# The K, V and Q projection of a hybrid decoder step as seven half-size products per column block

## What is computed

```python
def shared_kv(x, pos, g_kv, w_kv, k_gain):
    kv = jnp.einsum('btd,de->bte', rms_norm(x, g_kv), w_kv)
    kv = kv.reshape(B, T, 2, N_GROUPS, HEADS_PER_GROUP, HEAD_DIM)
    k = rotary(rms_norm(kv[:, :, 0], k_gain), pos)
    return k, kv[:, :, 1]
def project_q(x, pos, g, w_q, q_gain):
    q = jnp.einsum('btd,de->bte', rms_norm(x, g), w_q)
    return rotary(rms_norm(q, q_gain), pos) * (HEAD_DIM ** -0.5)
```

## Time and profile before

| | before |
|---|---|
| median of 3 runs | 2135.53 us (2135.42 to 2136.53) |
| span of the profiled execution | 2134.4 us |
| PE busy | 2106.5 us, 99% |
| DVE, ACT, POOL busy | 1533.9, 967.6, 559.0 us |
| projection on PE, first matmul to last | 766.66 to 1206.26 us |

### The profile page before, as it was taken

How to read it: one execution, slowest core, us unless ns; L and a number is a source line. 1 busy time by engine, 2 the same in 40 slices (tenths; PEclk the granted TensorE clock), 3 DMA queues, 4 the chain that set the end, 5 groups by cost and what they waited for, 6 DMA issues and landing times.

```text
span 2134.4 us, 42632 instructions
## 1 busy us (share of the span) xinstructions
PE 2106.5 (99%) x15883; PEld 1958.0 (92%) x15883; DVE 1533.9 (72%) x2321; ACT 967.6 (45%) x1797; POOL 559.0 (26%) x780
## 2 busy tenths in 40 slices
PE   7999999999999999999999999999999999999998
PEld 7999999999999987777777776899999999999998
DVE  4888888888755767457465588878888888875544
ACT  4655545555544542123122255645554554553342
POOL 1002232223100135455455301640213323311000
PEclk8999999999999999999999999999999999999999
DMA  6236777888986532432532785221567788899664
GB/s 195 90 95 161 199 198 193 207 193 234 300 276 195 181 110 85 158 100 84 169 114 93 228 243 159 70 90 55 155 191 196 193 210 195 198 291 303 194 209 142
DMA packets 237758, 371.02 MB, mean 174 GB/s; under 512 B 23687, under 2 KB 120615, under 8 KB 235734
## 3 DMA queue, kind: packets, MB, share of 16 engines
q1 hardware_dynamic: 196806, 258.73, 36.9%
q0 software_dynamic: 34960, 104.33, 22.0%
q10 hardware_dynamic: 5864, 6.25, 0.9%
HBM read 297.75 MB, written 168.07 MB: 218 GB/s over the span
## 4 chain that ended last, share of the span: by engine, by line
PE 95%; DVE 2%; ACT 1%; issue 0%; DMA 0%; POOL 0%; ACTq 0%; SPq 0%; DVEq 0%; POOLq 0%
PE ps L1255 42%; PE ps L1358 20%; PE ps L2164 6%; PE ps L2166 6%; PE ps L2165 6%; PE ps L2364 2%; PE ps L2434 2%; PE ps L2466 1%; PE ps L2447 1%; PE ps L424 1%; PE ps L2397 1%; PE ps L866 1%; PE ps L490 1%; PE ps L2426 1%; PE ps L2158 1%; PE ps L2159 1%
## 5 line engine op out<-in xcount | busy, mean ns | idle before, releaser
L1255 PE MATMUL ps<-hT,w 128*128 128x258 f32 x2752 | 458.2, 283 | 0.0
L1255 PEld LDWEIGHTS ps<-hT,w 128*128 128x128 f32 x2752 | 384.8, 189 | 0.5 <-ACT acc L1189 0.4
L1255 PE MATMUL ps<-lT,w 128*128 128x258 f32 x1376 | 276.3, 282 | 0.0
L1255 PE MATMUL ps<-hB,w 128*128 128x258 f32 x1344 | 229.3, 282 | 0.0
L2164 PE MATMUL ps<-wq,xh 128*128 128x512 f32 x576 | 227.6, 395 | 0.7 <-DVE wq L1948 0.7
L2166 PE MATMUL ps<-wq,xl 128*128 128x512 f32 x576 | 227.4, 395 | 0.0
L2165 PE MATMUL ps<-wq,xh 128*128 128x512 f32 x576 | 226.9, 394 | 0.0
L1255 PEld LDWEIGHTS ps<-lT,w 128*128 128x128 f32 x1376 | 213.3, 189 | 0.0
L1358 PE MATMUL ps<-gdh,wda 128*128 128x258 f32 x1184 | 198.8, 283 | 0.0
L1358 PE MATMUL ps<-gdh,wdb 128*128 128x258 f32 x1152 | 193.5, 284 | 0.1
L1255 PEld LDWEIGHTS ps<-hB,w 128*128 128x128 f32 x1344 | 191.0, 189 | 0.0
(11 more groups left out here) (350 smaller groups left out, 4714.7 us busy)
## 6 DMA issues: line engine op xcount, KB each, us to landing
stage<-in_w_up SPq DMA_DIRECT2D x176, 256.0 KB, 3.7
wsum<-in_w_down POOLq DMA_DIRECT2D x132, 256.0 KB, 5.3
gs<-cb SPq DMA_DIRECT2D x44, 516.0 KB, 7.0
stage<-wsum SPq DMA_DIRECT2D x88, 256.0 KB, 2.9
tsum<-gs POOLq DMA_DIRECT2D x66, 258.0 KB, 7.7
tsum<-gneg POOLq DMA_DIRECT2D x66, 258.0 KB, 8.4
stage<-in_w_down SPq DMA_DIRECT2D x58, 256.0 KB, 3.2
stage<-in_w_kv SPq DMA_DIRECT2D x24, 512.0 KB, 4.3
```

Of the source, the lines that this page charges most:

```text
L1255: mm = pe.matmul(ps[:, bank + c, 0:HB], w, m[:, c * HB:(c + 1) * HB], start=(first and i == 0), stop=(i == len(parts) - 1), skip_group_che ...
```

## The change

The projection becomes nine steps, PSTEPS, over (group, k or q or v), with the groups in order 1, 2, 0. In a step the 1024 prompt rows x 1024 inputs, and the 1024 x 512 weight block, are cut in quadrants (x into A11 to A22 of 512 rows x 512 inputs, the weights into B11 to B22 of 512 inputs x 256 columns), and seven products of half size are formed from them and from their sums S1 to S4 and T1 to T4 (the Winograd form of Strassen's scheme). A product is 4 row tiles x 4 x 3 matmuls of 256 columns, into two PSUM banks. The samples are multiplied straight, by 32 matmuls of 256 columns per step, in four pieces of eight, with the pieces of w that are in the ring anyway.

The order of the products is B11, T1, T2, B21, T3, T4, B22, and no product of step n + 1 stands before B22 of step n. Partial results move between banks as they are needed: `act_e1` copies banks 0-1 to 2-3 behind B11, `act_u2` and `act_u3` copy banks 2-3 to SBUF behind T2 and T3, and `dve_c22p`, `dve_c12p` add those copies to banks 4-5. T4 accumulates into banks 2-3 and so waits for u3; T1 of the next step starts banks 4-5 afresh and so waits for c12p. Four units of 512 rows x 256 columns (c11, c22, c21, c12) and one of the samples (S) come out of a step and are normed, rotated and stored as before, but in pieces of 128 x 1024. c22 comes out in the step; S, c21 and c12 are worked on in the next.

The sums of x are made in place by POOL (`pool_x_sum`) while the last FFN products run; x is therefore spilled to DRAM first, and loaded again during attention. Three weight slots (ring0 to ring2) rotate. In the first step PE also multiplies two matmuls of 512 columns that nothing reads. In a v step, DVE takes the sample scores 0 to 5 in that step and 6 and 7 in the next. The first tiles that the attention needs are turned by PE within the last step (`pe_first_turn`). Several semaphores are merged, which changes nothing of the order. The core of the diff:

```diff
         MT = [P] * 8 + [NS]
+        CW = QW // 2
+        GORDER = (1, 2, 0)
+        PSTEPS = [(g, u) for g in GORDER for u in range(3)]
+        LASTP = len(PSTEPS) - 1
+        ORDER_IN = ("B11", "T1", "T2", "B21", "T3", "T4", "B22")
+        PARTNER = {"B11": "A11", "T1": "S1", "T2": "S2", "B21": "A12", "T3": "S3", "B22": "S4", "T4": "A22"}
+        BANK = {"B11": 0, "B21": 0, "T1": 4, "B22": 4, "T2": 2, "T3": 2, "T4": 2}
+        UNITS = ("c11", "c22", "S", "c21", "c12")
+        BIG = ("c11", "c22", "c21", "c12")
...
+        def unit_made(n, name):
+            return {"c11": (pj_cp, 5 * n + 3), "c21": (pj_cp, 5 * n + 5), "c22": (pj_cs, 2 * n + 1),
+                    "c12": (pj_cs, 2 * n + 2), "S": (pj_k, 4 * n + 4)}[name]
...
+        def act_e1(act, n):
+            if n:
+                act.wait_ge(pj_cp, 5 * n)
+            else:
+                act.wait_ge(pj_ss, 1)
+            act_wide(act, ps[:, 2:4, :], ps[:, 0:2, :], (pj_pe, nth(n, "B11")))
+
+        def act_u2(act, n):
+            act.wait_ge(*((pj_cs, 2 * n) if n else (pj_ss, 2)))
+            act_wide(act, two(acc[:, 0:T]), ps[:, 2:4, :], (pj_pe, nth(n, "T2")))
+
+        def act_u3(act, n):
+            wait(act, pj_cs, 2 * n - 1)
+            act_wide(act, two(rb[:, 0:T]), ps[:, 2:4, :], (pj_pe, nth(n, "T3")))
...
+            for n in range(LASTP + 1):
+                last, normed = n == LASTP, PSTEPS[n][1] != 2
+                before = n and PSTEPS[n - 1][1] != 2
...
+                act_c11(act, n)
+                act_sample_low(act, n, 0)
+                if not last:
+                    act_scale(act, n + 1, "B12")
+                act_hi(act, n, "B22")
+                if normed and n:
+                    act_squares(act, n, "c11")
+                    act_root(act, n, "c11")
+                act_u3(act, n)
...
+                if not last:
+                    act_hi(act, n + 1, "B11")
+                    act_scale(act, n + 1, "B22")
+                if normed:
+                    act_squares(act, n, "c22")
+                    act_root(act, n, "c22")
...
+        def dve_c22p(v, n):
+            v.wait_ge(pj_cp, 5 * n + 4)
+            row_free(v, n, "c22")
+            nc.vector.tensor_tensor(two(row(n, "c22")), ps[:, 4:6, :], two(rb[:, 0:T]), ALU.add).then_inc(pj_cs, 1)
+
+        def dve_c12p(v, n):
+            v.wait_ge(pj_pe, nth(n, "B22"))
+            v.wait_ge(pj_cp, 5 * n + 2)
+            row_free(v, n, "c12")
+            nc.vector.tensor_tensor(two(row(n, "c12")), ps[:, 4:6, :], two(acc[:, 0:T]), ALU.add).then_inc(pj_cs, 1)
...
+            for n in range(LASTP + 1):
+                last, normed = n == LASTP, PSTEPS[n][1] != 2
+                before = n and PSTEPS[n - 1][1] != 2
+                gi = n // 3
+                if n:
+                    dve_weights_sum(v, n, "T2")
+                    dve_c12p(v, n - 1)
+                    dve_lo(v, n, "T2")
+                    if before:
+                        for name in ("S", "c21"):
+                            dve_mean(v, n - 1, name)
+                            dve_normed(v, n - 1, name)
+                        dve_lo(v, n, "B21")
+                        dve_weights_sum(v, n, "T3")
+                        dve_mean(v, n - 1, "c12")
+                        dve_normed(v, n - 1, "c12")
+                    else:
+                        for name in ("S", "c21"):
+                            dve_values(v, n - 1, name)
+                        dve_lo(v, n, "B21")
+                        dve_weights_sum(v, n, "T3")
+                        dve_values(v, n - 1, "c12")
+                        sample_scores(v, gi - 1, 6)
+                    dve_lo(v, n, "T3")
+                    dve_weights_sum(v, n, "T4")
+                    if not before:
+                        sample_scores(v, gi - 1, 7)
+                    dve_lo(v, n, "T4")
+                if not normed:
+                    dve_sample_add(v, n, 0)
+                    dve_values(v, n, "c11")
+                elif n:
+                    dve_lo(v, n, "B22")
+                    dve_mean(v, n, "c11")
+                    dve_sample_add(v, n, 0)
+                    dve_normed(v, n, "c11")
                 else:
...
+                    dve_sample_add(v, n, 0)
+                if not normed or n == 0:
+                    dve_lo(v, n, "B22")
+                dve_c22p(v, n)
+                if n == 0:
+                    dve_x_los("S4")
+                    dve_mean(v, n, "c11")
+                    dve_normed(v, n, "c11")
+                if not last:
+                    dve_lo(v, n + 1, "B11")
+                    dve_weights_sum(v, n + 1, "T1")
+                if normed:
+                    dve_mean(v, n, "c22")
+                    dve_normed(v, n, "c22")
+                else:
+                    dve_values(v, n, "c22")
+                    sample_scores(v, gi, 0)
+                    sample_scores(v, gi, 1)
+                if last:
+                    dve_masks(v)
+                    v.wait_ge(at_tp, 1)
+                    nc.vector.tensor_copy(qT[:, 0, :], ps[:, 6, :]).then_inc(at_tc, 1)
+                if not normed:
+                    sample_scores(v, gi, 2)
+                    sample_scores(v, gi, 3)
+                dve_sample_add(v, n, 1)
+                if last:
+                    v.wait_ge(at_tp, 2)
+                    nc.vector.tensor_copy(kT[:, 0, :], ps[:, 6, :]).then_inc(at_tc, 1)
+                else:
+                    dve_lo(v, n + 1, "T1")
+                if not normed:
+                    sample_scores(v, gi, 4)
+                    sample_scores(v, gi, 5)
+            dve_c12p(v, LASTP)
...
-                            pe.matmul(out, xh[:, k, tok], W, start=(k == 0), stop=False)
-                            pe.matmul(out, xh[:, k, tok], Wt, start=False, stop=False)
-                            mm = pe.matmul(out, xl[:, k, tok], W, start=False, stop=(k == KC - 1))
-                        mm.then_inc(pj_pe, 1)
...
+            def product(n, b):
+                pe.wait_ge(pj_l, nth(n, b))
+                if n == 0 or (n == 1 and b == "B11"):
+                    x_ready(b)
+                hi, lo = xq[PARTNER[b]]
+                w = wslot(n, b)
+                for t in range(KH):
+                    out = ps[:, BANK[b] + t // 2, t % 2 * CW:(t % 2 + 1) * CW]
+                    tok = slice(t * P, (t + 1) * P)
+                    for k in range(KH):
+                        cols = slice(k * CW, (k + 1) * CW)
+                        pe.matmul(out, hi[:, k, tok], w[:, 0, cols], start=(b in ("B11", "T1") and k == 0 and t % 2 == 0), stop=False,
+                                  skip_group_check=True)
+                        pe.matmul(out, hi[:, k, tok], w[:, 1, cols], start=False, stop=False, skip_group_check=True)
+                        mm = pe.matmul(out, lo[:, k, tok], w[:, 0, cols], start=False, stop=(k == KH - 1),
+                                       skip_group_check=True)
+                mm.then_inc(pj_pe, 1)
...
+            pe.wait_ge(f_xa, 6 * KH + 1)
+            for n in range(LASTP + 1):
+                if n:
+                    samples(n, "B11")
+                    pe.wait_ge(pj_cp, 5 * n - 2)
+                product(n, "B11")
+                if n == 0:
+                    pe.wait_ge(f_xa, 7 * KH)
+                    for c in range(2):
+                        pe.matmul(ps[:, 2 + c, :], xq["A11"][0][:, 0, 0:P], pre0[:, 0, 0:QW], start=True, stop=True)
+                    samples(0, "B11").then_inc(pj_ss, 1)
+                wait(pe, pj_cs, 2 * n)
+                product(n, "T1")
+                if n == 0:
+                    pe.wait_ge(split_acc, split[1].acc + 2 * KC - 2)
+                    for i in range(9):
+                        nm = pe.matmul(ps[0:MT[i], 7, i:i + 1], acc[:, i * P:i * P + MT[i]], ones[:, 0:1],
+                                       start=True, stop=True)
+                    nm.then_inc(pj_ss, 1)
+                pe.wait_ge(pj_cp, 5 * n + 1)
+                product(n, "T2")
+                samples(n, "B21")
+                product(n, "B21")
+                pe.wait_ge(pj_cp, 5 * n + 2)
+                product(n, "T3")
+                samples(n, "T3")
+                if n == LASTP:
+                    pe_first_turn(pe, 0)
+                pe.wait_ge(pj_cp, 5 * n + 4)
+                product(n, "T4")
+                samples(n, "B22")
+                if n == LASTP:
+                    pe_first_turn(pe, 1)
+                pe.wait_ge(pj_cs, 2 * n + 1)
+                product(n, "B22")
```

936 lines of the change are left out of this document (572 added, 364 removed).

## The result

| | before | after |
|---|---|---|
| median | 2135.48 us (4 runs, 2134.94 to 2136.53) | 2148.94 us (4 runs, 2146.43 to 2149.40) |
| ratio | 1 | 1.0063, 95% interval 1.0049 to 1.0078 |
| span of the profiled execution | 2134.4 us | 2144.6 us |

The account below looks back on a forecast made before the run. PE was taken as the bound, busy 2106.5 of 2134.4 us. Matmuls 400.2 + gates 10.2 + c12p 15.6 + step 8's end 8.0 + clock 5.1 = 439.1 against 439.6, so 2135.0 us; own forecast 2126 to 2144, range 2108 to 2160.

Parts of the forecast that it names:

- The matmuls: PE's projection: 3312 matmuls of 256 columns at 0.1197 us, 396.4 us, plus 3.8 of fixed parts, 400.2 without waits.
- the clock: PE at a lower clock after standing still: 1.7 us behind each long wait (after steps 2, 5, 8), 5.1 in all.
- My section on what costs nothing: Sums of x, spills and step 0's scaling fit under the last FFN products at no cost; up to 3 us if late.
- the waits for c12p behind v steps: T1 after steps 2 and 5 waits for c12p behind DVE's score rounds of 3.82 us: 7.8 us each, 15.6 in all.
- the end of step 8: Attention's start waits for DVE's scores, c12p and first maxima; PE loses 8.0 us, part already at the second turn.
- the gates: PE waits for u3 before T4: 0.3 us four times, 1.8 five times behind ACT's root, 10.2 in all.
- DVE does not set the pace in k and q steps: DVE needs 43.8 of a k or q step's 45.9 us, 8 for POOL's slowing included; only 2 us in hand.
- Waits of DVE are not on the path: Rival, chance 0.24: 15.6 + 8.0 + 5.1 us of waits and clock loss fall away, giving 2106 us; half gone, 2120.
- DVE and POOL block each other: Rival, chance 0.20: POOL's operations put up to 22 us per k or q step onto DVE; 2160 to 2194 us.
- short operations cost DVE nothing: Reading of the earlier trace: only POOL's one long operation delays DVE's two-input operations, by 1.3 us over four.
- the blocking would not reach PE: POOL's slowing, taken as 8 us per k or q step on DVE, fits within the step's 45.9 us.
- The third rival: Rival, chance 0.08: half-width matmuls slower, 0.125 us each, or last FFN products held up; 18 us more, 2153.

Follow-up runs that it names:

- four, no gain: Changed kernel with scores, u3, last-step order and earlier loads edited, and POOL's gain cut to 64 of 1024 columns (work left out): 2101.51 us, 0.9846 of before.
- the experiment on the scores: Changed kernel with sample scores 3 to 5 of steps 2 and 5 read after c12p, and c12p ahead of T2's sum: 2127.59 us, 0.9970 of before.
- fill: Changed kernel with 60 extra unused matmuls of 256 columns on PE ahead of T1 in steps 3 and 6: 2145.23 us, 1.0049 of before.
- last step: Changed kernel with qT, kT and c12p copies ahead of most scores in the last step, scores 2 to 7 between attention maxima: 2145.60 us, 1.0051 of before.
- no gain: Changed kernel with only POOL's gain multiplication cut to 64 of 1024 columns (work left out): 2134.09 us, 0.9993 of before.

## Why the prediction failed

**The matmuls** were right. With 2.4 us of waits left and no clock lost, "four, no gain" takes 400.8 us to the mask: 398.4 for matmuls and fixed parts, where my sum had 400.2. In the changed kernel that gives 398.4, plus the waits to 1210.50 (T1 19.9, gates 10.6, T2 2.0, turns 4.9, mask 1.1: 38.5), plus 9.8 of clock up to there: 446.7, against 446.6 measured.

**The waits** are where the prediction failed. Those that I forecast stand in the trace, at their places and with their releasers, and the experiment on the scores showed the largest by taking it away. But with the clock they are 38.9 us in my sum and 54.5 measured. These are the terms, against my 439.1 and a measured 446.6 + 6.3 (what the attention takes longer) = 452.9:

- the clock, 5.1 in the sum, 11.6 measured. I charged 1.7 once behind each of the three long waits, from the loss behind the norm's small matmuls; the two long ones cost 2.3 and 2.5, and 1.7 to 1.8 each were lost behind the projection's own small matmuls, a wait of 2.0 in step 1, a first turn that waited 2.1, and in the attention. By this count it is half of the miss, but not all of it cost time. T4 of step 1 starts 31.4 us behind T1 both in the changed kernel, with 1.7 us of clock lost between, and in the kernels of fill and last step, with none; there the gate waits 4.4 us in place of 2.9. The loss behind the first turn stands likewise ahead of the wait of 2.7 for qT, whose copy stood behind a score at 1200.62 that waited for POOL. Without these two the clock's loss is 8.2, and what it hid belongs to step 1 and the end of step 8.
- step 1. My section on what costs nothing had the work of step 0 under the FFN's last products; in fact DVE and ACT come out of it late, and PE waits 1.7 at T1 and 2.0 at T2: 3.7.
- the waits for c12p behind v steps, 15.6 in the sum, 18.2 measured. The rounds are shorter than I took, but the second score's buffer waits for a transfer of 6.3 us.
- the end of step 8, 8.0 in the sum; 6.0 ahead of the mask and 4.6 behind it, clock apart. Part of it is a transfer that I had not counted: the first q tile waits on SP's queue behind the store of c12.
- the gates, 10.2 in the sum, 10.6 measured, but for two reasons, not one: I had ACT's root alone, and the sum for T4 that POOL holds up was the other. That the total came out is luck: I had 1.8 in each of five steps, and they were 2.9, 1.4, 2.1, 1.4 and 2.1. Taking either reason away alone leaves 8.2 or 8.3; "four, no gain", which has both edits among its five, leaves 1.8.

Less 1.8 for the matmuls, that is 6.5 + 3.7 + 2.6 + 2.6 + 0.4 - 1.8 = 14.0, against 13.8.

One statement under the sum failed with it: that DVE does not set the pace in k and q steps. It is busy for 40.5 of the 46 us of step 4, and the last chain runs over it there.

**The rivals.** "Waits of DVE are not on the path" is refuted by the scores' edit. "DVE and POOL block each other" was right in kind and wrong in size. I took 8 us per k and q step on DVE, and 7.4 is what cutting the gain operation gave back. That short operations cost DVE nothing was a wrong reading of the earlier trace rows: beside those four operations of DVE, POOL's short ones took 0.79 and 0.77 us (from 868.65), and alone 0.46 and 0.32 (from 862.59), so each engine did wait for the other; and here a sum beside a short one takes 1.48 us for 1.2. My statement that the blocking would not reach PE failed too: with the gain operation cut away the kernels are 12 to 15 us faster, part of it through ACT's queue, part through POOL, which is free sooner. It would have had to be a term of the sum. The Trainium skill (SBUF — State Buffer, 🔬 SBUF: two separate sides) states exclusion for a whole instruction; this trace agrees, for long and short operations and with either engine waiting (3.44 us for a sum that takes 1.2 alone, ending 1.08 us behind POOL's). What these runs do not show is the rival's 22 us per step, nor would it follow from the rule of the Trainium skill: the rival counted every operation of POOL in full, where only DVE's two-input operations that meet one are held up. The third rival is refuted: the matmuls take no longer than forecast.

## What to carry to other kernels

A scheme that saves matmuls at the price of combinations moves the bound to whoever makes the combinations: look, for each wait that closes a step, at everything that stands ahead of the released instruction on its engine's queue, and put what the step doesn't need behind it. Here that was six small reductions, and moving three of them and one sum was worth 21 us, more than the change lost. When PE begins to wait, give the clock a range of its own, with waits of some 2 us in it, but count nothing for a loss that stands ahead of a wait whose end does not depend on PE, as in step 1; at the gate of step 3, whose end does, the 2.0 us stayed. Where two engines take turns, look at where an operation ends and not at how long it is recorded, since the length holds the wait. And test edits together as well as alone: one of five gained nothing alone and cost time in company.

## What the runs showed of the hardware

- The granted clock after short waits is not the same in each execution. Behind a wait of 1.7 us ahead of T1 in step 1 it fell to 0.53 in the scores' kernel and stayed 1.00 in the changed one; behind 2.1 us in step 4 it fell in the last step's kernel (0.50 at 1006) and not in the changed one. Of waits between matmuls of the projection, the 22 of 3.5 us or more (the shortest 3.56) all had the lower level behind them, and those of 1.5 us and below had not. With it the runs spread: the kernel before lies within 2132.8 and 2137.8 over 21 runs, "no gain" within 2127.3 and 2139.0 over 11. That the one causes the other was not tried.
- A query row, spread over all partitions, took 3.3 to 10.1 us from issue to landing in the changed kernel, with a median of 4.2. The slow ones were the first three of each v step: 6.3 us in the chain at 903.54, 8.2 in the last step (issued at 1186.78), longer than a whole round of the scores.
- An operation of DVE that reads two tensors of SBUF and one of POOL take turns as wholes in the changed kernel: the one that starts second ends a fixed time behind the end of the other, 1.08 us for a sum that takes 1.2 alone (24 of 26 cases) and 0.32 for POOL's short one. A reduction of DVE that reads one tensor keeps its 1.21 us beside POOL.
